# Gathered rows of a mixture-of-experts layer: dots on VectorE in three second layers, weighted sums on GpSimd

## The reference, cut to what matters

```python
def chunk(args):                       # hc: tokens, ec: their experts, gc: gates
    hc, ec, gc = args
    u = jnp.take(u_tab, ec, axis=0)    # a row of 2048 for each token and expert
    act = jax.nn.gelu(jnp.einsum('cd,ckd->ck', hc, u), approximate=False) * gc
    vv = jnp.take(v_tab, ec, axis=0)
    return jnp.einsum('ck,ckd->cd', act, vv)
```

## Time and profile before

| what | value |
|---|---|
| three timed runs | 3556.6, 3562.51, 3565.51 us (median 3562.51) |
| the profiled execution, its own time | 3553.24 us |
| its span in the trace | 3551.5 us |
| granted TensorE clock, mean | 0.984 |
| busy: TensorE matmul / VectorE / ScalarE / GpSimd | 3345.1 / 2556.5 / 1582.7 / 140.7 us |
| DMA | 658.20 MB, mean 185 GB/s |

### The profile page before, as it was taken

One profiled execution on the slowest core, in us unless ns is written; L12 is line 12 of the kernel. 1 busy time (PEld: TensorE's weight loads), 2 busy tenths in 40 slices (PEclk: granted clock), 3 DMA queues, 4 the chain that ended last, 5 costly groups with the idle time before them and its releaser, 6 DMA issues.

```text
span 3551.5 us, 68558 instructions
## 1 busy us (share of the span) xinstructions
PE 3345.1 (94%) x24838; PEld 2975.9 (84%) x24838; DVE 2556.5 (72%) x4414; ACT 1582.7 (45%) x2501; POOL 140.7 (4%) x122
## 2 busy tenths in 40 slices
PE   8999899999999899988879999899999999999998
PEld 6888788888888777777768788889989899989898
DVE  6767687777778787766766589776666767777786
ACT  5445444444444555433424313444444445454543
POOL 0000000000000000000000001000000000101000
PEclk9999999999999999999999999999999999999999
DMA  5544455555555444410005544676777677868674
GB/s 194 172 143 162 158 167 172 193 178 190 178 192 174 166 146 149 136 52 9 6 26 165 178 136 171 240 268 239 265 248 271 236 270 240 304 242 309 236 266 166
DMA packets 174996, 658.20 MB, mean 185 GB/s; under 512 B 19744, under 2 KB 28064, under 8 KB 165280
## 3 DMA queue, kind: packets, MB, share of 16 engines
q1 hardware_dynamic: 159744, 559.15, 47.0%
q0 software_dynamic: 15104, 97.03, 7.4%
HBM read 637.99 MB, written 17.04 MB: 184 GB/s over the span
## 4 chain that ended last, share of the span: by engine, by line
PE 72%; DVE 19%; ACT 5%; issue 2%; DMA 1%; ACTq 0%; DVEq 0%; SPq 0%
PE bank L608 40%; PE bank L610 20%; DVE w_lo L1970 7%; PE bank L946 5%; ACT w_hi L1325 3%; PE bank L1230 2%; DVE p_raw L2899 1%; DVE hot_row L2865 1%; DVE rows L2878 1%; DVE p_two L2905 1%; DVE stage L1980 1%; DVE hot_col L2860 1%; DVE h_tok L2886 1%; PE bank L631 1%; DVE proj L2528 1%
## 5 line engine op out<-in xcount | busy, mean ns | idle before, releaser
L608 PE MATMUL bank<-h_two,w_hi 128*128 128x512 f32 (+1 forms) x5360 | 1822.9, 391 | 78.7 <-DVE w_lo L1970 49.4
L610 PE MATMUL bank<-h_two,w_lo 128*128 128x256 f32 (+1 forms) x5360 | 1465.2, 273 | 0.0
L1970 DVE TENSOR_TENSOR w_lo<-raw,w_hi 128x1024 fp32r<-128x1024 f32 (+1 forms) x1054 | 1228.3, 1184 | 225.6 <-ACT w_hi L1325 224.0
L1325 ACT ACTIVATE w_hi<-raw 128x1024 fp32r<-128x1024 f32 (+1 forms) x1054 | 1045.8, 1024 | 481.4 <-PE bank L610 407.8
L608 PEld LDWEIGHTS bank<-h_two,w_hi 128*128 128x128 f32 x5360 | 1008.3, 188 | 270.8 <-DVE w_lo L1970 55.2
L610 PEld LDWEIGHTS bank<-h_two,w_lo 128*128 128x128 f32 x5360 | 1017.5, 190 | 1.1 <-issue 0.7
L608 PE MATMUL bank<-p_two,w_hi 128*128 128x448 f32 x1792 | 582.0, 382 | 23.0 <-DVE p_two L2905 21.4
L610 PE MATMUL bank<-p_two,w_lo 128*128 128x224 f32 x1792 | 481.7, 269 | 0.0
L608 PEld LDWEIGHTS bank<-p_two,w_hi 128*128 128x128 f32 x1792 | 343.3, 192 | 57.3 <-DVE p_two L2905 23.4
L610 PEld LDWEIGHTS bank<-p_two,w_lo 128*128 128x128 f32 x1792 | 349.3, 195 | 0.0
L608 PE MATMUL bank<-f_two,w_hi 128*128 128x512 f32 x704 | 250.9, 398 | 13.5 <-DVE f_two L2299 13.5
(11 more groups left out here) (401 smaller groups left out, 3306.9 us busy)
## 6 DMA issues: line engine op xcount, KB each, us to landing
raw<-in_u_tab SPq DMA_DIRECT2D x256, 512.0 KB, 4.7
raw<-in_v_tab SPq DMA_DIRECT2D x256, 512.0 KB, 4.7
raw<-in_w_up SPq DMA_DIRECT2D x176, 512.0 KB, 5.4
raw<-in_w_in SPq DMA_DIRECT2D x174, 512.0 KB, 3.9
raw<-in_w_out SPq DMA_DIRECT2D x64, 512.0 KB, 5.2
raw<-in_w_down SPq DMA_DIRECT2D x64, 512.0 KB, 3.5
raw<-in_w_pq SPq DMA_DIRECT2D x32, 512.0 KB, 4.2
gates<-g_stage POOLq DMA_DIRECT2D x14, 896.0 KB, 6.0
```

Source lines behind the costliest of these rows:

```text
L608: nc.tensor.matmul(o[:, 0:2 * width].rearrange("p (a t) -> p a t", a=2), wh, pair[:, :, 0:width], start=(k == 0), stop=False)
L610: last = nc.tensor.matmul(o[:, width:2 * width], wl, pair[:, 0, 0:width], start=False, stop=(k == nk - 1))
L1325: nc.scalar.activation(w_hi[c % 2][:, at:end], raw[c % 2][:, at:end], ACT.Copy).then_inc(hi_done, 1)
L1970: nc.vector.tensor_tensor(w_lo[c % 2][:, at:end], raw[c % 2][:, at:end], w_hi[c % 2][:, at:end].bitcast(F32), ALU.subtract).then_inc(lo_do ...
```

## The change

`OPS_IN` now gives rows of VectorE to the second layers of g = 0, 1 and 2 alone, 10, 11 and 11 of them, which are the 32 dots; a row comes behind a single chunk (`rows_behind(g, t)`). The 32 sums are GpSimd's own work: `added_rows(n)` multiplies a row by its weight in place (one instruction) and adds it to `y_tok` (a second one, behind a semaphore of its own). `SUMS_IN` puts 11, 11 and 10 of them behind the loads of `g_now` for groups 4, 5 and 6, that is, from the end of the first layers of g = 3, 4 and 5 on. The gelu of the dots and the multiplication by the gates come one group earlier. The first chunk of a second layer waits for tile 14 of 16 at its first matmul and for the last two tiles at the two pairs that read them.

```diff
--- before.py
+++ after.py
@@ -123,7 +123,8 @@
 GATHERS = SLOTS // KQ
 
 
-OPS_IN = (4, 4, 4, 4, 4, 4, 4, 4, 4, 7, 4, 7, 4, 6)
+OPS_IN = (0, 10, 0, 11, 0, 11)
+SUMS_IN = {4: 11, 5: 11, 6: 10}
 ROWS_USED = [sum(OPS_IN[:i]) for i in range(len(OPS_IN) + 1)]
 
 
@@ -1288,9 +1289,9 @@
             def expert_values(c, g, p):
                 def p_ready(k):
                     if k == 0:
-                        pe.wait_ge(p_lo_done, g * DT + (DT - 1))
-                    if k == DT - 1:
-                        pe.wait_ge(p_lo_done, g * DT + DT)
+                        pe.wait_ge(p_lo_done, g * DT + (DT - 2))
+                    if k >= DT - 2:
+                        pe.wait_ge(p_lo_done, g * DT + (k + 1))
                 chunk(c, g * DT, p, DT, p_ready, whole=WHOLE, width=TD)
                 chunk(c + 1, g * DT, p, whole=WHOLE, width=TD)
                 with pe.Fori(1, DT // 2) as i:
@@ -1863,12 +1864,12 @@
 
             first_layer(0)
             second_splits(0)
-            with act.Fori(1, 4) as g:
+            with act.Fori(1, 3) as g:
                 first_layer(g)
                 second_splits(g)
             act.wait_ge(rows_used, GATHERS)
             nc.scalar.activation(act_of[:], dots[:], ACT.Gelu).then_inc(gate_exp, 1)
-            with act.Fori(4, PEER_G - 2) as g:
+            with act.Fori(3, PEER_G - 2) as g:
                 first_layer(g)
                 second_splits(g)
             g = PEER_G - 2
@@ -1949,17 +1950,35 @@
                 gather(n)
             for j in range(2):
                 pool.wait_ge(gates_stored[j], 16 * (TD // 32))
-            begun = 2
+
+            def added_rows(n):
+
+                pool.wait_ge(rows_loaded[n % 2], 16 * (n // 2 + 1))
+                pool.wait_ge(rows_used, n)
+                got, of = rows[n % 2][:], n % GATHERS
+                if of == 0:
+                    pool.wait_ge(best_ready, 2)
+                    last = nc.gpsimd.tensor_scalar(y_tok[:], got, act_of[:, 0:1], None, ALU.mult)
+                else:
+                    nc.gpsimd.tensor_scalar(got, got, act_of[:, of:of + 1], None, ALU.mult).then_inc(pool_set, 1)
+                    pool.wait_ge(pool_set, 2 + of)
+                    last = nc.gpsimd.tensor_tensor(y_tok[:], y_tok[:], got, ALU.add)
+                last.then_inc(rows_used, 1)
+
+            begun, summed = 2, GATHERS
             for g in range(1, PEER_G):
-                while begun < 2 * GATHERS and begun < ROWS_USED[2 * g - 1] + 2:
+                while begun < GATHERS + 2 and begun < ROWS_USED[min(2 * g - 1, len(OPS_IN))] + 2:
                     gather(begun)
                     begun += 1
 
                 pool.wait_ge(stage_used, g * DT + S_PEER)
                 pool.dma_start(g_now[:], gates_d[g]).then_inc(g_loaded, 16)
-            while begun < 2 * GATHERS:
-                gather(begun)
-                begun += 1
+                for n in range(SUMS_IN.get(g, 0)):
+                    if begun < 2 * GATHERS and begun < summed + 2:
+                        gather(begun)
+                        begun += 1
+                    added_rows(summed)
+                    summed += 1
 
         @block.vector
         def _(dve):
@@ -2874,25 +2893,17 @@
                 got, of = rows[n % 2][:], n % GATHERS
                 if n == 0:
                     dve.wait_ge(k_swapped, 32 + (3 * KQ - 1) * 16)
-                if n < GATHERS:
-                    last = nc.vector.tensor_tensor_reduce(got, got, h_tok[:], 1.0, 0.0, ALU.mult, ALU.add,
-                                                          dots[:, of:of + 1])
-                else:
-                    dve.wait_ge(rows_used, n)
-                    if of == 0:
-                        dve.wait_ge(best_ready, 2)
-                        last = nc.vector.tensor_scalar(y_tok[:], got, act_of[:, 0:1], None, ALU.mult)
-                    else:
-                        last = nc.vector.scalar_tensor_tensor(y_tok[:], got, act_of[:, of:of + 1], y_tok[:],
-                                                              ALU.mult, ALU.add)
+                last = nc.vector.tensor_tensor_reduce(got, got, h_tok[:], 1.0, 0.0, ALU.mult, ALU.add,
+                                                      dots[:, of:of + 1])
                 last.then_inc(rows_used, 1)
 
-            def rows_behind(x, i):
-
-                at = ROWS_USED[x]
-                for n in range(at, ROWS_USED[x + 1]):
-                    if (n - at) * 8 // OPS_IN[x] == i:
-                        gathered_rows(n)
+            def rows_behind(g, t):
+
+                if 2 * g + 1 < len(OPS_IN):
+                    at = ROWS_USED[2 * g + 1]
+                    for n in range(OPS_IN[2 * g + 1]):
+                        if n * DT // OPS_IN[2 * g + 1] == t:
+                            gathered_rows(at + n)
 
             def gated(i, j, g):
                 dve.wait_ge(gelu_done, g * DT + i * 2 + (FFN_Q * FQT + j + 1))
@@ -2915,10 +2926,9 @@
                         gated(i, j, g)
                         lower(N_PEER + DT + j + 2, g * DT + i, whole=WHOLE)
                         gated_lower(i, j, g, p_hi[:, i * 2 + j, :], p_lo[:, i * 2 + j, :])
-                    if g == 4 and i == 0:
+                    if g == 3 and i == 0:
                         dve.wait_ge(gate_exp, 2)
                         nc.vector.tensor_tensor(act_of[:], act_of[:], gate_of[:], ALU.mult).then_inc(best_ready, 1)
-                    rows_behind(2 * g, i)
 
             def second_layer(c, g, i, j, next_part=True):
                 it = g * DT + i
@@ -2936,7 +2946,7 @@
                 for i in range(DT // 2):
                     for j in range(2):
                         second_layer(N_PEER + 2 * DT, g, i, j)
-                    rows_behind(2 * g + 1, i)
+                        rows_behind(g, i * 2 + j)
             g = PEER_G - 2
             first_layer(g)
             dve.wait_ge(g_loaded, (g + 1) * 16)
```

## The result

The change takes 3658.99 us (median, 3654.96 to 3664.25) against 3560.93 us for the kernel before: the ratio is 1.0276, with a 95% interval of 1.0257 to 1.0295. It is slower by 98 us. The profiled execution of the change took 3664.25 us with a span of 3662.5 us. The forecast was 3622 us, slower by 60, with a range from 3512 to 3690.

A forecast was written before the change was run, and what follows sets the result against it. TensorE was taken as the bound, waiting 53.6 us in 1200. Rows and join -47, dots 0, GpSimd sums +107 make +60 us on 3562.5: forecast 3622 us, range 3512 to 3690.

The forecast's parts named there:

- Rows out of the first layers, and the join, -47 us: First layers and joins: 21 `w_lo` waits go, -30.6 us, and the join's wait shrinks, -16 us; together -47 us.
- 16 us of the 47: Start of each second layer: the `p_two` wait falls from 3.06 us on average to about 0.75, -16 us.
- Dots in three second layers, 0: Second layers with dots: VectorE's lateness stays below the 3.5 us of cover and the gathers fit; costed at 0.
- Rival C (DMA): Layers with dots: no lock that matters, but DMA limits at 310 GB/s; +42 against -47, 3557 us, chance 0.06.
- I take it that the exclusion is mutual: Second layers with sums: GpSimd and VectorE instructions shut each other out and take turns; +107 us for the sums.
- Rival B: Second layers with sums: VectorE isn't shut out, so the -47 us stand; 3516 us, chance 0.30.
- D: Second layers with sums: GpSimd is slow, above 14.7 us a row, without shutting VectorE out; about 3623 us, chance 0.06.
- I take 2.0 ... and 4.4: GpSimd's sums: multiplication 2.0 us and addition 4.4, estimated from a memset; 6.4 us a row.
- over 9: GpSimd's sums: a row under 4.5 us or over 9 was named as a sign that the prediction is wrong.
- One row goes with one chunk, which takes ... 8.84 us: Second layers with sums: two instructions and two `w_lo` halves take 8.84 us instead of 5.07; 117 us for 31 rows.
- the prediction's own formula: Whole change: 31 x (r + 2.44 - 5.07) - 10 - 47, with r GpSimd's time for a row.
- The rows fit ... so the first layers stay free of them: Second layers with sums: 10 or 11 rows fit in 16 chunks, and `g_now` isn't late.

The follow-up runs named there:

- Experiment 1: The change with its 32 sums back on VectorE, 8 in each second layer of groups 3 to 6: 3506.25 us, ratio to the kernel before 0.9851.
- experiment 2: The kernel before with the new join alone (14 tiles at the first matmul, the last two pairs wait for theirs): 3551.95 us, ratio 0.9982.
- experiment 3: Experiment 1 with the old join put back (15 tiles at the first matmul): 3505.03 us.
- experiments 4 and 5: The kernel before plus a tail timing GpSimd arithmetic, 3652.11 us; and the change with six memsets replacing 31 rows' multiplication and addition, sums left out, 3508.36 us.

## Why the prediction was right, and which term was mis-sized

The sign, the mechanism and its place were right, the size was too small: +60 forecast, +98 measured. By the steps:

- *Rows out of the first layers, and the join, -47 us.* Experiment 1 gives -53.5. The waits of TensorE over groups 0 to 6 fell from 53.6 to 9.0 us there, nearly as said, and in the change the join came down to 0.77 us (0.75 forecast):

```profile
2347.22 0.47 PE L609 MATMUL bank<-p_two,w_hi 128*128 128x448 f32 x1 [0.77 <-DVE p_two L2916]
```

  What the sum left out is the low clock behind each join of 3 us, 14 us by the estimate of experiment 2. The prediction had seen a clock of 0.98 in the second layer of g = 4 and called that layer one without waits; but the 0.98 is its join: 0.70 in the first 5.5 of 81.3 us gives just that. It put at most 11 us on the clock, in the first layers, and left them out of the sum. And 16 us of the 47 were credited to the new join, which experiment 3 shows to be worth nothing once the rows are gone. At the three joins that GpSimd's work begins on, the wait is 3.8 to 4.2 us, since the last lower tile stands behind a multiplication (`p_two` L2916 lasts 3.84 us there instead of 0.38): the forecast had none of these 10 us.
- *Dots in three second layers, 0.* Right. DMA went to 342 GB/s at a share of 0.94, and TensorE waited 5.2 us up to the first sum. Rival C (DMA) fell.
- *"I take it that the exclusion is mutual."* Right, shown by the change's own trace and experiments 4 and 5. The Trainium skill (SBUF — State Buffer, Who interferes with whom) was right in naming two SBUF inputs against a reading GpSimd, and that writing doesn't count; its "fully blocks" for the whole instruction nearly holds for the addition (a half of `w_lo` begun just behind its start lasts 4.1 us longer, of 4.5) but not for the multiplication (3.6 of 5.4). Rival B fell; D would have needed a row of over 14.7 us, and it takes 12.73.
- *"I take 2.0 ... and 4.4."* This is the step that failed. The addition alone takes 4.50 us, as estimated, and as the 4497 ns of the Trainium skill (GPSIMD Engine Reference, 3.1 Elementwise). The multiplication takes 5.45, outside the 1.76 to 3.5 derived from a memset: a memset (1.80) was no measure for an instruction that reads. A row is 9.95 us alone and 10.6 beside VectorE, where the prediction had named "over 9" as a sign of being wrong.
- *"One row goes with one chunk, which takes ... 8.84 us."* A chunk takes 8.49 us, near it, but by two errors that cancel in part: the row is longer than forecast, and three halves of `w_lo` pass in its 12.73 us, not two. A row holds VectorE up for 4.3 + 4.1 = 8.4 us and spoils one and a half chunks: 12.73 - 1.5 x 5.07 = 5.1 us lost, not 3.77. With the measured 9.95 us in the prediction's own formula it would have been 31 x (9.95 + 2.44 - 5.07) - 10 - 47 = +170 us, 3732 us and outside the range. That the forecast came as near as it did is partly luck.
- *"The rows fit ... so the first layers stay free of them."* Nearly: 11 rows of 12.73 us are 140 us, longer than the layer of 130, and the last one of g = 4 runs on into the next first layer, where TensorE waits 5.2 us.

With the term at 31 x 5.1 - 10 = +149 (measured between experiment 1 and the change: 153) and experiment 1's -53.5 the sum is +95.5; measured are 98. That is closer than the terms are known: the 10 us at the joins are not in it, and what takes them back was not looked into.

## What to carry to other kernels

Before work is moved to GpSimd because VectorE is busy, count which of VectorE's instructions have two inputs in SBUF: each of them waits behind a GpSimd instruction that reads SBUF, for 2.7 to 4.3 us in the rows above, with 2048 elements, while instructions with one input in PSUM beside it, and GpSimd's memsets, cost nothing. Here the whole gain, 53.5 us, came from moving VectorE's own rows from a serial loop with 0.05 us to spare (the first layers) to layers with 2.1 us to spare, and VectorE could take the sums there too. A busy share doesn't show this: look at the loop's round time against TensorE's chunk.

## What the runs showed that I had not expected

- A multiplication by a scalar on GpSimd is slower than an addition of two tensors, 5.45 against 4.50 us for 128x2048 in float32, and a memset takes 1.80.
- Longer waits of TensorE were often followed by the lower clock, and that costs beyond the wait. After the change's wait of 3.84 us the granted clock is 0.50 in the stretch from 1.6 us on, and back at 0.99 after about 4 us:

```profile
2842.00:2843.60 1.60, 1.55 (x7) 1.48 (x8) 0.94 (x2) 0.94 (x1) 1.56 (x2) 0.71 0.89 305
2843.60:2846.00 2.40, 2.40 (x10) 2.23 (x9) 2.40 (x1) 0.12 (x1) 2.40 (x1) 0.50 0.70 224
2846.00:2850.00 4.00, 4.00 (x26) 3.78 (x26) 3.58 (x5) 1.06 (x1) 3.92 (x2) 0.99 0.92 374
```

  The length of the wait alone doesn't decide it. In experiment 2 one join in seven was followed by it after 1.7 us, and in the change a wait of 3.33 us wasn't:

```profile
2898.80:2904.30 5.50, 5.29 (x32) 4.75 (x32) 5.50 (x3) 1.06 (x1) 5.35 (x2) 1.00 0.57 192
```

  At the joins one wait of 3 us came out dearer than two that sum to nearly the same, which is likely most of what the new join bought in experiment 2.
- A half of `w_lo` that begins during a gather may have to wait for what follows the gather: in the change one begins 0.7 us ahead of the multiplication's recorded start and is held all the same, where in the earlier trace rows one that began in a gather with nothing behind it took its 1.23 us. The traces don't tell whether GpSimd's reading begins before the start that they show.
